# A five-place ring for the experts' up-projections, and the last state tile's products on another engine

## The reference

```python
# state-space mixer: a complex diagonal recurrence over the 256 tokens, 64 groups x 64 states
bu = einsum('sbgk,gpk->sbgp', ut, bb)          # real and imaginary part
_, _, xr, xi = lax.associative_scan(combine, (ar_t, ai_t, bu_re, bu_im), axis=0)
y = einsum(xr, c_re) - einsum(xi, c_im)
...
# mixture of experts: the best 2 of 8 for each token, D = 1024, EXPERT_FF = 2816
logits = h @ w_router
top_val, top_idx = lax.top_k(logits, 2)
gates = sum(one_hot(top_idx, 8) * softmax(top_val)[..., None], axis=-2)
for e in range(8):
    out = out + gates[..., e:e+1] * ((silu(h @ w_gate[e]) * (h @ w_up[e])) @ w_down[e])
```

## Time and profile before

| | |
|---|---|
| median of 3 runs | 2010.81 us (2009.47 to 2020.08) |
| the profiled execution | 2012.9 us, span of the core 2011.1 us |
| TensorE busy | 1931.3 us, 96% of the span |
| mean granted TensorE clock | 0.981 of full speed |
| mixture of experts | from 1217 us to about 2000 us of the span |
| bytes moved | 483.96 MB |

### The profile page before, as it was taken

How to read it: one execution, slowest core, us unless ns; L and a number is a source line. 1 busy time by engine, 2 the same in 40 slices (tenths; PEclk the granted TensorE clock), 3 DMA queues, 4 the chain that set the end, 5 groups by cost and what they waited for, 6 DMA issues and landing times.

```text
span 2011.1 us, 28485 instructions
## 1 busy us (share of the span) xinstructions
PE 1931.3 (96%) x11940; PEld 1067.7 (53%) x11940; DVE 689.8 (34%) x1472; ACT 372.2 (19%) x776; POOL 114.9 (6%) x98
## 2 busy tenths in 40 slices
PE   8999999999998999999989899999999999999998
PEld 6577866678856666777666453233332323232322
DVE  3364323374323662544379832010101010111112
ACT  3322113222113231343220021010101010101001
POOL 0000000000000000000036600000000000000000
PEclk9999999999999999999999898999999999999999
DMA  9255564345554317343223146989898989898993
GB/s 350 107 204 230 221 264 172 148 193 240 217 237 167 126 63 269 129 178 136 82 86 126 42 199 250 353 347 363 346 388 342 371 339 377 339 376 325 406 367 153
DMA packets 44036, 483.96 MB, mean 241 GB/s; under 512 B 5108, under 2 KB 6772, under 8 KB 10328
## 3 DMA queue, kind: packets, MB, share of 16 engines
q1 hardware_dynamic: 39136, 471.73, 59.1%
q10 hardware_dynamic: 4248, 9.07, 1.3%
q0 software_dynamic: 576, 2.10, 0.3%
HBM read 479.07 MB, written 10.10 MB: 243 GB/s over the span
## 4 chain that ended last, share of the span: by engine, by line
PE 84%; DMA 8%; DVE 5%; issue 1%; ACT 1%; ACTq 1%; SPq 0%; POOL 0%; DVEq 0%
PE bank L911 18%; PE bank L569 14%; PE bank L941 11%; PE bank L864 8%; DMA arena<-in_wgu 6%; PE bank L876 4%; PE bank L728 3%; PE bank L561 3%; PE bank L554 3%; PE bank L734 3%; PE bank L582 2%; PE bank L990 2%; DMA arena<-bias_rows 1%; PE bank L1085 1%; PE bank L550 1%; PE bank L1018 1%
## 5 line engine op out<-in xcount | busy, mean ns | idle before, releaser
L911 PE MATMUL bank<-arena 128*32 128x512 f32 x4096 | 467.5, 603 | 20.7 <-DMA arena<-in_wgu 20.6
L569 PE MATMUL bank<-arena 128*128 128x256 f32 x1408 | 314.2, 382 | 0.0
L911 PEld LDWEIGHTS bank<-arena 128*32 128x32 f32 x4096 | 134.0, 111 | 335.0 <-issue 306.0
L569 PEld LDWEIGHTS bank<-arena 128*128 128x128 f32 x1408 | 266.3, 191 | 54.4 <-issue 15.8
L941 PE MATMUL bank<-arena 128*32 128x512 f32 x2112 | 238.2, 595 | 0.0
L2067 DVE TENSOR_TENSOR arena<-arena,bank 128x256 f32<-128x256 f32 x64 | 27.0, 421 | 594.2 <-ACT arena L1437 543.6
L864 PE MATMUL bank<-arena 128*128 128x256 f32 x704 | 153.7, 379 | 0.1
L864 PEld LDWEIGHTS bank<-arena 128*128 128x128 f32 x704 | 133.6, 190 | 21.8 <-issue 4.1
L941 PEld LDWEIGHTS bank<-arena 128*32 128x32 f32 x2112 | 62.9, 109 | 133.4 <-issue 132.7
L1437 ACT ACTIVATE arena<-bank 128x256 f32<-128x256 f32 x64 | 24.6, 385 | 549.6 <-PE bank L911 549.5
L2313 POOL TENSOR_TENSOR arena<-arena 128x512 f32<-128x512 f32 x64 | 81.2, 1269 | 293.4 <-DVE arena L2121 290.9
(11 more groups left out here) (446 smaller groups left out, 1892.9 us busy)
## 6 DMA issues: line engine op xcount, KB each, us to landing
arena<-in_wgu SPq DMA_DIRECT2D x88, 2048.0 KB, 10.9
arena<-in_w SPq DMA_DIRECT2D x46, 2048.0 KB, 7.6
arena<-in_wdn SPq DMA_DIRECT2D x88, 1024.0 KB, 8.1
arena<-in_modw SPq DMA_DIRECT2D x24, 2048.0 KB, 9.4
arena<-in_wf SPq DMA_DIRECT2D x11, 3072.0 KB, 10.5
arena<-in_flt_deltas ACTq DMA_DIRECT2D x2, 1024.0 KB, 12.2
slot_rows<-arena ACTq DMA_DIRECT2D x7, 192.0 KB, 3.3
cst<-in_consts SPq DMA_DIRECT2D x1, 1162.0 KB, 7.7
```

What stands on the lines that cost most here:

```text
L569: ins = mm(bank[b][:, j * S:(j + 1) * S], w[:, col:col + P], hT[:, k, :], start=(k == 0), stop=(k == KT - 1))
L911: ins = mm(bank[w % 2][32 * j:32 * j + 32, :], hTe[:, k, TOK * b:TOK * b + TOK], wslot[c % RING][:, k, :], start=(k == 0), stop=(k == KT - ...
```

## The change

The up tiles get a fifth place, and the order of SyncE's loads changes. Place 4 lies where `taken` was (the rows that are gathered back for the last item), and `taken` is split over four other regions that are free at that time. Chunks go to places 0, 1, 2, 3, 4, 0, 1, 2, 3, 4, 2. `TURN` is how often a place was used before in the item, `OUSTED` the chunk that had it last.

Independently of that, the two table products of state tile 31 move from GpSimd to VectorE, right behind the tile's scans and ahead of `y_tile(6)`. GpSimd's loop stops after tile 30, and `s5_out(30)` waits for both.

```diff
+UP = RING + 1
+SLOT = [0, 1, 2, 3, 4, 0, 1, 2, 3, 4, 2]
+TURN = [SLOT[:c].count(SLOT[c]) for c in range(FFC)]
+UP_USES = [SLOT.count(r) for r in range(UP)]
+OUSTED = [max(p for p in range(c) if SLOT[p] == SLOT[c]) if TURN[c] else max(p for p in range(FFC) if SLOT[p] == SLOT[c])
+          for c in range(FFC)]
...
-        wslot = [view(CH * r, KT, 512) for r in range(RING)]
+        wslot = [view(CH * r, KT, 512) for r in range(RING)] + [view(W + 10752, KT, 512)]
...
-        taken = view(W + 10752, 2, TT, D)
+        taken = [[view(W + 4416, D), view(W + 5440, D)], [view(W + 14848, D), view(W + 18432, D)]]
...
-                if c >= RING:
-                    sp.wait_ge(sm["xh_ps"], i * WAVES + (more * WAVES + LAST[c - RING] + 1))
+                if TURN[c]:
+                    sp.wait_ge(sm["xh_ps"], i * WAVES + (more * WAVES + LAST[OUSTED[c]] + 1))
                 elif more:
-                    sp.wait_ge(sm["xh_ps"], i * WAVES + (LAST[PREV[c]] + 1))
+                    sp.wait_ge(sm["xh_ps"], i * WAVES + (LAST[OUSTED[c]] + 1))
...
-                for load, c in ((load_up, 4), (load_up, 5), (load_up, 6), (load_down, 4), (load_up, 7), (load_down, 5),
-                                (load_down, 6), (load_up, 8), (load_down, 7), (load_up, 9), (load_up, 10)):
+                for load, c in ((load_up, 5), (load_up, 6), (load_up, 7), (load_up, 8), (load_down, 4), (load_up, 9),
+                                (load_down, 5), (load_down, 6), (load_down, 7)):
                     load(i, e, c, more)
...
             for c in range(2):
                 load_up(0, 0, c)
+            load_up(0, 0, 4)
             load_down(0, 0, 0)
...
                 e0 = sp.value_load(itab[0:1, bass.ds(i, 1)], min_val=0, max_val=EXPERTS - 1)
                 e = sp.value_load(itab[0:1, bass.ds(i + 1, 1)], min_val=0, max_val=EXPERTS - 1)
+                load_up(i, e, 0, 1)
+                load_up(i, e, 1, 1)
+                load_up(i, e0, 10)
+                load_down(i, e0, 8)
                 load_up(i, e, 3, 1)
-                load_down(i, e0, 8)
-                load_up(i, e, 0, 1)
                 load_down(i, e0, 9)
                 load_down(i, e0, 10)
-                load_up(i, e, 1, 1)
                 load_up(i, e, 2, 1)
+                load_up(i, e, 4, 1)
                 load_down(i, e, 3, 1)
                 for c in range(3):
                     load_down(i, e, c, 1)
                 middle(i, e, 1)
             e = sp.value_load(itab[0:1, bass.ds(last, 1)], min_val=0, max_val=EXPERTS - 1)
+            load_up(last, e, 10)
             for c in (8, 9, 10):
                 load_down(last, e, c)
...
-                pe.wait_ge(sm["cz_ready"], o + 2)
+                pe.wait_ge(sm["cz_ready"], min(o + 2, STATE_TILES - 1))
+                if o + 2 == STATE_TILES:
+                    pe.wait_ge(sm["z5_ready"], STATE_TILES + 1)
...
+                if i == STATE_TILES - 1:
+
+                    dve.wait_ge(sm["sy_ps"], i - 3)
+                    for n in range(2):
+                        ins = v.tensor_tensor(cz[i % 4][:, n], zz[:, i % 2],
+                                              tab[i][:, n, :].unsqueeze(1).broadcast_to([P, 2, S]), ALU.mult)
+                        if n == 0:
+                            link(ins)
+                    ins.then_inc(sm["z5_ready"], 1)
...
-            for o in range(STATE_TILES):
+            for o in range(STATE_TILES - 1):
                 pool.wait_ge(sm["z5_ready"], o + 1)
```

More of the change, by code:

```diff
@@ L363, in model @@
                             for k in ("ffn", "s5"))
-        landedw = landed
+        landedw = landed + [ctx.enter_context(nc.semaphore("landed_up"))]
         landedd = landedf
@@ L436, in load_up @@
             def load_up(i, e, c, more=0):
-                if c >= RING:
-                    sp.wait_ge(sm["xh_ps"], i * WAVES + (more * WAVES + LAST[c - RING] + 1))
+                if TURN[c]:
+                    sp.wait_ge(sm["xh_ps"], i * WAVES + (more * WAVES + LAST[OUSTED[c]] + 1))
                 elif more:
-                    sp.wait_ge(sm["xh_ps"], i * WAVES + (LAST[PREV[c]] + 1))
-                sp.dma_start(wslot[c % RING].rearrange("p a b -> p (a b)"), a["wgu"][e * FFC + c])\
-                    .then_inc(landedw[c % RING], 16)
+                    sp.wait_ge(sm["xh_ps"], i * WAVES + (LAST[OUSTED[c]] + 1))
+                sp.dma_start(wslot[SLOT[c]].rearrange("p a b -> p (a b)"), a["wgu"][e * FFC + c])\
+                    .then_inc(landedw[SLOT[c]], 16)
             def load_down(i, e, c, more=0):
@@ L889, in lone @@
                     c, b = LONE
-                    pe.wait_ge(landedw[c % RING], i * (16 * USES[c % RING]) + (earlier + 16 * (c // RING + 1)))
+                    pe.wait_ge(landedw[SLOT[c]], i * (16 * UP_USES[SLOT[c]]) + ((earlier if SLOT[c] < RING else 0) + 16 * (TURN[c] + 1)))
                     for k in range(KT):
                         g = k % 4
-                        ins = mm(bank[3][32 * g:32 * g + 32, :], hTe[:, k, TOK * b:TOK * b + TOK], wslot[c % RING][:, k, :],
+                        ins = mm(bank[3][32 * g:32 * g + 32, :], hTe[:, k, TOK * b:TOK * b + TOK], wslot[SLOT[c]][:, k, :],
                                  start=(k < 4), stop=(k >= 4), skip_group_check=True)
@@ L911, in wave @@
                             ins = mm(bank[w % 2][32 * j:32 * j + 32, :], hTe[:, k, TOK * b:TOK * b + TOK],
-                                     wslot[c % RING][:, k, :], start=(k == 0), stop=(k == KT - 1), skip_group_check=True)
+                                     wslot[SLOT[c]][:, k, :], start=(k == 0), stop=(k == KT - 1), skip_group_check=True)
                     ins.then_inc(sm["xh_ps"], 1)
@@ L2213, in rows_added @@
                     for n, gate in enumerate((30, 36)):
-                        link(v.scalar_tensor_tensor(x[:, t, :], taken[:, n, t, :], small[:, gate + t:gate + t + 1], x[:, t, :],
+                        link(v.scalar_tensor_tensor(x[:, t, :], taken[n][t], small[:, gate + t:gate + t + 1], x[:, t, :],
                                                     ALU.mult, ALU.add))
@@ L2323, in _ @@
                     at = ITEMS + 2 + 2 * n + t
-                    pool.indirect_dma_start(out=taken[:, n, t, :], out_offset=None, in_=table,
+                    pool.indirect_dma_start(out=taken[n][t], out_offset=None, in_=table,
                                             in_offset=bass.IndirectOffsetOnAxis(ap=itab[:, at:at + 1], axis=0))\
```

## The result

The changed kernel takes 1983.59 us (median of 4 runs, 1981.42 to 1989.14); the kernel before 2012.05 (median of 4, the three of the table above and one more). The ratio is 0.9864, 95% interval 0.9841 to 0.9886, so some 27 us less, with 23 to 32 in the interval. It is the shortest of the four, which reach to 1989.14; so the two ways of measuring, 27 and 31.5 us, are no contradiction.

A forecast was written before the change was run, and what follows sets the result against it. The prediction took TensorE, busy 96% of the span, as the bound, gains coming from its waits and lost clock. Terms -30.1 - 1.2 + 1 = -30.3 us gave 1982.6 us for the profiled execution, 1980 for the median, range 1975 to 1993.

The forecast's parts named there:

- The waits of wave 5 and their clock: TensorE's waits for up tiles, nearly all in wave 5: -20.4 us, -9.5 us of lost clock, -0.2 in wave 2; -30.1 us.
- Why chunk 8 was late: SyncE's queue: up 8 stood behind down 5 and down 6, issued 6.5 us after its place was free, landing 10.95 later.
- What is late next: up 10: Up 10, used in wave 7, becomes tight behind down 7 and the next item's up 0 and up 1; 0.5 to 2.7 us left.
- The bounds of 19.6 to 21.8 us: Time needed from down 7's issue until up 10 has landed, against 22.3 us available before wave 7.
- The reads at the loop's top: Two item-table reads between down 7 and up 0, 0.28 us each: no gap in transfers, or one of some tenths.
- 1 us for waits: Up 10's waits before wave 7: 0.1 us an item, +1 us in all; ends 0 and 1.3 us an item.
- The last state tile: State tile 31's two products on VectorE, 1.45 us against 2.60: TensorE starts 1.2 us earlier, its following matmuls still slow.
- That the transfers are the bound: Rival: 355 to 363 GB/s over whole items is all the memory gives; waits only move, 2010 us, no change; chance 5%.
- That the clock would not come back: Rival: wave 5 stays slow without a wait, the gain is 9.5 us less, 1990 us; chance 4%.
- the tie: Rival: up 10 makes wave 7 wait 2.5 us, with 1.7 of clock, eating the gain; 2013 us, no change; chance 2%.

The follow-up runs named there:

- e5_down8: The changed kernel with up 10 behind down 8 in SyncE's order; ratio to the kernel before 0.9888, experts' stage 766.8 us.
- e4_late: The changed kernel with up 10 issued one wave later, waiting for wave 6 in place of wave 5; ratio to the kernel before 1.0009, experts' stage 795.6 us.
- e3_tile: The kernel before with only the last state tile's two products moved to VectorE; ratio to the kernel before 1.000.
- e1_order: The kernel before, four places, with up 8 moved ahead of down 5 and down 6; ratio to the kernel before 0.9879, experts' stage 767.2 us.
- e6_sorted: The kernel before, four places, with its loads from up 4 on in the order of their releases; ratio to the kernel before 0.9869, experts' stage 761.8 us.
- e9_up7: The kernel before, four places, with only up 7 moved ahead of down 4; ratio to the kernel before 0.988, experts' stage 770.1 us.
- e7_place: The changed kernel, fifth place kept, with up 8 behind down 4, down 5 and down 6 again; ratio to the kernel before 0.9892, experts' stage 765.2 us.

## Why the prediction was right

**The waits of wave 5 and their clock** (-30.1 us forecast, -32.3 us in the stage). The mechanism and the place were right. The sum was 2 us short: in item 3 the clock was never lost, and still its length fell from 96.25 to 94.02 us (from one L900 or L910 to the next), 2.23 us for a wait of 1.85. Some tenths more go with each wait than the idle time shows. `e5_down8` has the same: 3.6 us of waits in seven times, and 5.4 us more in the stage, which is 0.26 us for each. With 0.26 for nine waits the forecast would have been 32.4; the same sum gives 34.8 for `e4_late`, where 34.2 was measured, and 35.6 for `e3_tile`, where its stage is 35.5 us above 761.4. Where the tenths go is not shown. For the profiled execution the forecast was 1982.6 us, and 1981.42 came; for the median 1980, and 1983.59 came, with executions of the changed kernel that differ by 8 us among themselves.

**Why chunk 8 was late.** The prediction saw one cause, the order: up 8 issued 6.5 us after its place was free. `e1_order` and `e6_sorted` show that this suffices. It also read the 10.95 us that up 8 then took to land, and did not ask for their cause: 9 would have done, and 9 it was when up 7 went out 3.7 us sooner (`e9_up7`). Since the lateness was only 1.9 to 3.8 us, either cure, alone, removes most of it: the order 31.9 us, the place 28.5. Their gains don't add, and the whole has 32.3. For the forecast it made no difference, as the change does both.

**What is late next: up 10.** The bounds of 19.6 to 21.8 us from down 7's issue, against 22.3 us there were, fit what can be worked out for item 3. There, after the change, down 7 went out at 1457.7, and then these three, the next item's up 0 and up 1 at 1460.0 and 1460.6, and up 10:

```profile
L448 SPq DMA_DIRECT2D arena<-in_wgu x3: 332/333/336, 1460.0 to 1464.6; - x3
DMA to landing us min/median/max: 8.0/10.2/12.4
```

The trace has no landing for up 10, so the times are those of the first two. Up 1 was in at 1460.6 + 12.4 = 1473.0, and up 10 should be 4.9 us later by the rate, at about 1477.9. That is 20.2 us after down 7's issue, and 1.9 us before wave 7 at 1479.82, in agreement with `e5_down8`. The reads at the loop's top put up 0's issue 2.3 us behind down 7's, and opened no gap in the transfers, as forecast. They run at 427 GB/s from 1460 on:

```profile
1460.00:1478.00 18.00, 18.00 (x168) 5.32 (x164) 0.84 (x2) 1.44 (x4) 0.00 (x0) 1.00 1.01 427
```

The forecast had put aside 1 us for waits; there were none.

**The last state tile.** -1.2 us forecast, -1.13 by the wait, and the low clock stayed, as assumed. What of it reaches the end lies below the scatter.

**The rivals.** That the transfers are the bound is refuted by the stage after the change: it moves 372 to 373 GB/s in the mean of an item, more than the 355 to 363 that would have been the limit.
The Trainium skill's limit of about 358 GB/s for one core ("DMA: Bandwidth & Descriptors", section Bandwidth) is passed by this mean over whole items as well.
That the clock would not come back is refuted by 7.05 to 7.08 us in every wave 5 after. The price that the tie was given, a wait of 2.5 us with 1.7 of clock, is near what `e4_late` measured: 2.8 us of wait an item, the clock lost in six of eight, and a ratio of 1.0009.

## What to carry to other kernels

When several loads with different releases share one issuing queue, write down for each its release, its issue and its landing, and compare them with its first use. Putting them in the order of their releases costs no memory, and should be tried before another buffer. A load can be late because its issue waits behind others, or because it takes long to land behind loads that were issued before it. The first is seen by its issue beside its release, the second by its time to landing beside the shortest of the same size (8.0 to 8.6 us here for 2 MiB with little or nothing ahead). TensorE's waits of 2 to 3 us cost about one and a half times their length here (20.6 us of waits and 32.3 in the stage; 22.5 and 34.2 in `e4_late`), with the clock; so look at the instructions behind a wait, too.

## What the runs showed of the hardware

A wait's length alone doesn't say whether the granted clock falls. In the experts' stages of this study all waits for up tiles of 2.01 us and less kept it, and most above lost it, but 2.35 us in `e3_tile` and 2.86 and 2.87 us in `e4_late` kept it (7.07 and 7.08 us for the wave behind them), while 2.16 and 2.17 us lost it. What else decides was not tried.

With transfers always queued the rate was 427 GB/s; a second 2 MiB load queued right behind a first landed 4.9 to 5.0 us after it. What makes a load take longer is in part open. In item 3 before, down 5 was issued 2.0 us before up 7 landed and took 6.5 us, where it took 4.8 to 4.9 in `e9_up7` and `e7_place` with no byte moving when it was issued. But in the changed kernel up 0 was issued 2.6 us before down 7 landed, and took 8.0 us, against 7.9 for the quickest up tile of that trace. So a load that is still coming in doesn't by itself make the next one late; what differs was not tried.
